# A hybrid decoder step on one core: seven of twelve pairs of expert weight chunks stored as 32 KB rows and loaded by one 4 MB transfer each

## The reference

```python
xn  = rmsnorm(x)
mix = x + (sum_i sigmoid(gate_i) * (branch_i @ w_br_i)) @ w_o    # three branches from xn @ w_in
xn2 = rmsnorm(mix)
grp = argmax(xn2 @ w_rg + b_rg)            # one of 4 groups
top2 of the 8 experts of the group, weight = p(group) * softmax(top2 logits)
for each of 32 experts e:
    h    = silu(xn2 @ w_gate[e]) * (xn2 @ w_up[e])     # 2048 -> 512
    out += (h * combine[:, e]) @ w_down[e]             # 512 -> 2048
y = rmsnorm(mix + out)
```

## Time and profile before

| | |
|---|---|
| time, median of 3 runs | 1625.97 us (1625.96 to 1627.1) |
| span of the profiled execution | 1624.0 us |
| PE busy | 1412.6 us, 87% |
| DVE, ACT busy | 563.5 us, 408.6 us |
| DMA moved | 544.69 MB, mean 335 GB/s |
| chain that ended last | DMA 49%, PE 48% |

### The profile page before, as it was taken

The page is one execution under the profiler, slowest core; times in us unless marked ns, Lnnn a source line. Parts: engine busy times, 40 slices in busy tenths (PEclk is TensorE's granted clock), DMA queues, the critical chain, the costliest instruction groups (busy, mean ns, idle before and its releaser), DMA issues.

```text
span 1624.0 us, 24618 instructions
## 1 busy us (share of the span) xinstructions
PE 1412.6 (87%) x10019; PEld 931.0 (57%) x10019; DVE 563.5 (35%) x924; ACT 408.6 (25%) x684; POOL 29.9 (2%) x52
## 2 busy tenths in 40 slices
PE   7999999999999999999877777877878867967866
PEld 7999999999999999953322322322312412412311
DVE  5647765554455555442111111112111111201204
ACT  6454344333333344321201101002002002002003
POOL 0100020000000010000000000000000000000000
PEclk9999999999999999999989989989889989989989
DMA  8776555545555558699999999999999999999997
GB/s 334 291 299 240 168 164 182 182 158 203 181 181 181 194 218 354 240 360 423 428 426 429 429 426 428 429 429 427 428 428 429 428 427 429 428 427 429 429 427 307
DMA packets 53022, 544.69 MB, mean 335 GB/s; under 512 B 6289, under 2 KB 6337, under 8 KB 11609
## 3 DMA queue, kind: packets, MB, share of 16 engines
q1 hardware_dynamic: 51442, 539.26, 82.1%
q0 software_dynamic: 1392, 4.78, 1.1%
q10 hardware_dynamic: 144, 0.02, 0.0%
HBM read 540.30 MB, written 3.68 MB: 335 GB/s over the span
## 4 chain that ended last, share of the span: by engine, by line
DMA 49%; PE 48%; DVE 1%; ACT 1%; issue 0%; SPq 0%; DVEq 0%; ACTq 0%
DMA trunk<-in_expert_chunks 27%; DMA ring<-in_expert_chunks 18%; PE bank L1468 13%; PE bank L1469 13%; PE bank L1470 13%; PE bank L1860 4%; DMA side<-in_expert_chunks 3%; PE bank L1863 1%; DMA ring<-in_dense_units 1%; PE bank L1746 1%; PE bank L1630 0%; PE bank L1792 0%; DMA trunk<-in_mem_cols 0%; PE bank L1800 0%; PE bank L1664 0%
## 5 line engine op out<-in xcount | busy, mean ns | idle before, releaser
L940 DVE TENSOR_TENSOR w_lo<-ring,w_hi 128x1024 fp32r<-128x1024 f32 x220 | 259.8, 1222 | 223.2 <-ACT w_hi L673 222.7
L1468 PE MATMUL bank<-xn_hi,w_hi 128*128 128x264 f32 x1120 | 319.0, 285 | 0.0
L1469 PE MATMUL bank<-xn_lo,w_hi 128*128 128x264 f32 x1120 | 317.3, 283 | 0.0
L1470 PE MATMUL bank<-xn_hi,w_lo 128*128 128x264 f32 x1120 | 317.1, 283 | 0.0
L673 ACT ACTIVATE w_hi<-ring 128x1024 fp32r<-128x1024 f32 x220 | 221.1, 1052 | 366.5 <-PE bank L1470 333.1
L1468 PEld LDWEIGHTS bank<-xn_hi,w_hi 128*128 128x128 f32 x1120 | 210.9, 188 | 1.1 <-issue 1.0
L1469 PEld LDWEIGHTS bank<-xn_lo,w_hi 128*128 128x128 f32 x1120 | 211.1, 188 | 0.1
L1470 PEld LDWEIGHTS bank<-xn_hi,w_lo 128*128 128x128 f32 x1120 | 210.0, 187 | 0.0
L1860 PE MATMUL bank<-ring,trunk 128*32 128x512 f32 x896 | 125.6, 685 | 55.4 <-DMA ring<-in_expert_chunks 55.4
L1860 PE MATMUL bank<-side,trunk 128*32 128x512 f32 x832 | 118.7, 694 | 58.1 <-DMA side<-in_expert_chunks 56.7
L1746 PEld LDWEIGHTS bank<-trunk,x_all 128*128 128x128 f32 (+1 forms) x672 | 93.3, 192 | 75.7 <-issue 55.8
(11 more groups left out here) (324 smaller groups left out, 1730.7 us busy)
## 6 DMA issues: line engine op xcount, KB each, us to landing
ring<-in_expert_chunks SPq DMA_DIRECT2D x79, 2048.0 KB, 37.0
side<-in_expert_chunks SPq DMA_DIRECT2D x72, 2048.0 KB, 36.3
ring<-in_dense_units SPq DMA_DIRECT2D x109, 1024.0 KB, 4.8
trunk<-in_expert_chunks SPq DMA_DIRECT2D x24, 2048.0 KB, 36.9
trunk<-in_expert_chunks SPq DMA_DIRECT2D x16, 1024.0 KB, 38.8
side<-in_expert_chunks SPq DMA_DIRECT2D x16, 1024.0 KB, 40.8
x_all<-in_k_cols SPq DMA_DIRECT2D x8, 512.0 KB, 7.7
x_all<-in_cache_mem_v SPq DMA_DIRECT2D x8, 512.0 KB, 6.6
```

The lines of the kernel that those rows point to most:

```text
L940: V.tensor_tensor(w_lo[n % 2][:, js, :], raw[n % 2][:, js, :], w_hi[n % 2][:, js, :], ALU.subtract).then_inc(lo_done, 1)
L1468: mm(ps[:, 0:n], w_hi[b][:, j, :], x_hi[:, j, :], start=j == k0, stop=False)
L1469: mm(ps[:, 0:n], w_hi[b][:, j, :], x_lo[:, j, :], start=False, stop=False)
L1470: ins = mm(ps[:, 0:n], w_lo[b][:, j, :], x_hi[:, j, :], start=False, stop=j == k1 - 1)
```

## The change

On the host, the two chunks of seven pairs of each round (0 and 1, 4 and 5, 6 and 7, 8 and 9, 12 and 13, 16 and 17, 20 and 21) are interleaved by partition: in HBM a partition's 16 KB of one chunk are followed by its 16 KB of the other, so a pair is 128 rows of 32 KB. Their two slots lie side by side in SBUF (for the pairs with the value 1 in `PAIRS` in the reverse order), and one transfer of 128 x 32 KB fills both. It is issued when the second of the two earlier chunks is used, since it overwrites both. PE waits once, before the first chunk of a pair, for the whole pair. The other ten chunks of a round are loaded as before, and so are five places in the first round: chunk 4, the halves of 5, chunks 6, 7, 8 and 9 come singly, as 16 KB or 8 KB pieces out of the 32 KB rows. The pair 0, 1 of the first round is one transfer at k = 3; nothing is issued at k = 5 any more.

The diff:

```diff
--- before.py
+++ after.py
@@ -57,8 +57,10 @@
 CREDIT = 8
 SLOT = [EORDER[c % 8] for c in range(CPR)]
 SLOT[14], SLOT[15], SLOT[22], SLOT[23] = 8, SLOT[6], SLOT[7], 8
-REFILL = [(p, p + 8) for p in range(6)] + [(None, 14), (6, 15)] + [(p, p + 8) for p in range(8, 14)] + [(None, 22), (14, 23)]
-AHEAD = [(16 + c, c) for c in range(6)] + [(None, 6), (22, 7)]
+PAIRS = {0: 0, 4: 1, 6: 0, 8: 0, 12: 1, 16: 0, 20: 1}
+SECOND = {c + 1: c for c in PAIRS}
+REFILL = [(1, 8), (2, 10), (3, 11), (5, 12), (None, 14), (6, 15), (9, 16), (10, 18), (11, 19), (13, 20), (None, 22), (14, 23)]
+AHEAD = [(17, 0), (18, 2), (19, 3), (21, 4), (22, 6)]
 SP_STEPS = (0, 6, 7, 8, 14, 15, 16, 22, 23)
 
 
@@ -366,6 +368,7 @@
         e_used, p_ready, p_step, silu_done, h_ready, y_ready = (
             sem("e_used"), sem("p_ready"), sem("p_step"), sem("silu_done"), sem("h_ready"), sem("y_ready"))
         sq_done, f_var, f_sqrt, f_rms = sem("sq_done"), sem("f_var"), sem("f_sqrt"), sem("f_rms")
+        first4_in, first6_in, first8_in = sem("first4_in"), sem("first6_in"), sem("first8_in")
         half_full, acc2_in, shift_ok, spread_ok = sem("half_full"), sem("acc2_in"), sem("shift_ok"), sem("spread_ok")
         g_ready, g_taken, half0_full = sem("g_ready"), sem("g_taken"), sem("half0_full")
         first_turned, first_taken = sem("first_turned"), sem("first_taken")
@@ -383,14 +386,16 @@
 
         def expert_full(c):
 
-            return sum(32 if k == 14 else 16 for k in range(c + 1) if SLOT[k] == SLOT[c])
+            return sum(32 if k == 14 else 16 for k in range(c + 1) if SLOT[k] == SLOT[c] and k not in SECOND)
 
         def slot_fills(c):
 
-            return expert_full(max(k for k in range(CPR) if SLOT[k] == SLOT[c]))
+            return expert_full(max(k for k in range(CPR) if SLOT[k] == SLOT[c] and k not in SECOND))
 
         units_v = dense_units.rearrange("m p n -> p m n")
         chunk_v = expert_chunks.rearrange("r c p n -> p c r n")
+        pair_v = expert_chunks.rearrange("r (q t) p n -> r q (t p n)", t=2).rearrange("r q (p m) -> p q r m", p=P)
+        pair_slot = {4: view(side, 4096, 2 * CHUNK), 1: view(ring, 0, 2 * CHUNK), 3: view(ring, UNIT0, 2 * CHUNK)}
 
         raw = [view(ring, b * KT * P, KT, P) for b in range(2)]
 
@@ -478,12 +483,24 @@
                              chunk_v[:, c, round_of, jj * (CHUNK // 2):(jj + 1) * (CHUNK // 2)]).then_inc(
                                  half_full if c == CPR - 1 and jj else full[8], 16)
 
+            def from_pair(c, round_of, n0, n1):
+
+                c0 = SECOND.get(c, c)
+                at = (c - c0 ^ PAIRS[c0]) * CHUNK
+                return pair_v[:, c0 // 2, round_of, at + n0:at + n1]
+
+            def one_of_pair(c, round_of, signal):
+
+                sp.dma_start(e_slot[SLOT[c]].rearrange("p (o n) -> p o n", o=1), from_pair(c, round_of, 0, CHUNK)).then_inc(signal, 16)
+
             def expert_load(c, round_of):
 
                 s = SLOT[c]
                 if s == 8:
                     half_load(c, 0, round_of)
                     half_load(c, 1, round_of)
+                elif c in PAIRS:
+                    sp.dma_start(pair_slot[s].rearrange("p (o n) -> p o n", o=1), pair_v[:, c // 2, round_of, :]).then_inc(full[s], 16)
                 else:
                     sp.dma_start(e_slot[s].rearrange("p (o n) -> p o n", o=1), chunk_v[:, c, round_of, :]).then_inc(full[s], 16)
 
@@ -504,20 +521,22 @@
                     if k == 2:
                         sp.wait_ge(x_zero, 1)
                         sp.dma_start(g_row, g_final.rearrange("(o n) -> o n", o=1)).then_inc(gfin_in, 16)
-                    if 3 <= k < 3 + 2 * EARLY and k % 2:
-                        expert_load(k // 2 - 1, slice(0, 1))
+                    if k in (3, 7, 9):
+                        expert_load({3: 0, 7: 2, 9: 3}[k], slice(0, 1))
+                    if k == 11:
+                        one_of_pair(4, slice(0, 1), first4_in)
 
             sp.wait_ge(aux_ready, A_O + KT - 4)
             sp.wait_ge(lg_ready, KT // 2 - 2)
             residual(KT - 2)
-            for half, signal in ((0, half0_full), (1, full[SLOT[EARLY]])):
+            for half, signal in ((0, half0_full), (1, full[SLOT[4]])):
                 sp.wait_ge(*lo_after(N_OUT + 14 + half))
                 cols = slice(half * (CHUNK // 2), (half + 1) * (CHUNK // 2))
                 sp.dma_start(e_slot[SLOT[EARLY]][:, cols].rearrange("p (o n) -> p o n", o=1),
-                             chunk_v[:, EARLY, slice(0, 1), cols]).then_inc(signal, 16)
-            for c in (1, 2):
-                sp.wait_ge(z_ready, Z_END + c - 2)
-                expert_load(EARLY + c, slice(0, 1))
+                             from_pair(EARLY, slice(0, 1), cols.start, cols.stop)).then_inc(signal, 16)
+            for c, signal in ((6, first6_in), (7, full[SLOT[6]])):
+                sp.wait_ge(z_ready, Z_END + c - 7)
+                one_of_pair(c, slice(0, 1), signal)
             half_load(14, 0, slice(0, 1))
             sp.wait_ge(aux_ready, A_LT + 1)
             half_load(14, 1, slice(0, 1))
@@ -536,7 +555,11 @@
                     expert_load(c, of_round)
 
             with sp.Fori(0, npass) as k:
-                refill(REFILL, k * (ROUNDS * CPR) + CREDIT, slice(0, 1), 14)
+                sp.wait_ge(e_used, k * (ROUNDS * CPR) + (CREDIT + 1))
+                one_of_pair(8, slice(0, 1), first8_in)
+                sp.wait_ge(e_used, k * (ROUNDS * CPR) + (CREDIT + 2))
+                one_of_pair(9, slice(0, 1), full[SLOT[8]])
+                refill(REFILL[1:], k * (ROUNDS * CPR) + CREDIT, slice(0, 1), 14)
                 refill(AHEAD, k * (ROUNDS * CPR) + CREDIT, slice(1, 2))
                 with sp.Fori(1, ROUNDS - 1) as r:
                     refill(REFILL, k * (ROUNDS * CPR) + r * CPR + CREDIT, bass.ds(r, 1))
@@ -1764,6 +1787,7 @@
             pe.wait_ge(np_ready, 1)
             npass = pe.value_load(npass_i[0:1, 0:1], min_val=1, max_val=9)
             pe.wait_ge(half0_full, 16)
+            pe.wait_ge(first4_in, 16)
             pe.wait_ge(first_taken, 1)
             with pe.Fori(0, npass) as k:
                 with pe.Fori(0, ROUNDS) as r:
@@ -1845,7 +1869,12 @@
                                 ins = tr(ps[:, j * P:(j + 1) * P], h[:, j, :], ident[:, :])
                             ins.then_inc(aux_ready, 1)
                             pe.wait_ge(aux_done, it * JPR + (A_E + JOB_H + 1))
-                        pe.wait_ge(full[SLOT[c]], it * slot_fills(c) + expert_full(c))
+                        if c == 6:
+                            pe.wait_ge(first6_in, 16)
+                        if c == 8:
+                            pe.wait_ge(first8_in, k * 16 + 16)
+                        if c not in SECOND:
+                            pe.wait_ge(full[SLOT[c]], it * slot_fills(c) + expert_full(c))
                         for jj in range(2):
                             w = weights(SLOT[c], jj)
                             if jj and c < 8:
@@ -1876,6 +1905,18 @@
          (1, 8, 1, 768)]
 
 
+def interleave_pairs(out):
+
+    import numpy as np
+
+    for c, last_first in PAIRS.items():
+        both = out[:, c:c + 2].transpose(0, 2, 1, 3)
+        if last_first:
+            both = both[:, :, ::-1]
+        out[:, c:c + 2] = np.ascontiguousarray(both).reshape(ROUNDS, 2, P, CHUNK)
+    return out
+
+
 def pack_experts(w_gate, w_up, w_down):
 
     import numpy as np
@@ -1887,7 +1928,7 @@
         into[:, 8 * i:8 * i + 8] = w.transpose(0, 2, 4, 3, 1, 5)
     w = np.asarray(w_down).reshape(ROUNDS, EPR, 2, 2, P, 4, 512)
     into[:, 16:].reshape(ROUNDS, 4, 2, P, 2, EPR, 512)[:] = w.transpose(0, 5, 2, 4, 3, 1, 6)
-    return out
+    return interleave_pairs(out)
 
 
 def columns(*rows):
```

## The result

The changed kernel takes 1630.53 us (median of 16 runs), the kernel before 1626.01 us (16 runs): a ratio of 1.0031 with a 95% interval of 1.0024 to 1.0037. It is slower by 4.5 us. The forecast was 1628.7 within 1623.8 to 1632.8, with 0.45 on slower by over 0.2%.

The account below looks back on a forecast made before the run. PE was taken to bound the kernel up to 700 us, DMA streaming from about 730. Terms +1.05 +1.45 -3.5 +2.6 +1.1 = +2.7 us took the span from 1624.0 to 1626.7, median 1628.7 us, range 1623.8 to 1632.8.

Parts of the forecast that it names:

- The other signs: Expected in the new profile: 117.1 us rounds; last half of chunk 23 without a wait, ending 14.6 us after pair 20, 21.
- case 1: The forecast itself: four small terms, three of them losses, nearly cancel; 1628.7 us, own range 1627.0 to 1630.5, chance 0.55.
- What a byte costs: Expert stream: 32 KB rows and one transfer save 0.07 us per pair, 50 pairs, -3.5 us, bounds 0 and -5.5.
- Rival 2: Each of the 50 pairs: a long row saves nothing, leaving losses of +6.2 us, 1632.2 us; chance 0.2.
- rival 4: Expert stream: longer rows stream slower, 0.1 us lost on each of 53 pairs, +11.5 us, 1637.5 us; chance 0.05.
- The dense part: Unit at k = 4 lands later behind 4 MB and PE stalls once, +1.05 us, bounds 0 and 2.
- The dry gaps: First round: pairs 12, 13 and 16, 17 are issued later, DMA runs dry twice, +1.45 us, bounds 0.8 and 2.
- The later rounds: After the first round: later issue of pairs costs nothing, since five or six chunks are still queued.
- Rival 5: Later rounds: DMA runs dry there too, at 1 us per pair, 1680 us; chance 0.03.
- The tail: Last round: PE has more work after pair 20, 21 lands, +2.6 us; slower clock after idling, +1.1, bounds 0 and +2.
- Rival 3: Losses smaller than worked out and 32 KB rows save 0.11 us: 1622 to 1624 us or little more; chance 0.15.
- rival 6: The change does not do what it says, each pair moves as before; in time like Rival 2; chance 0.02.

Follow-up runs that it names:

- rows16: Changed kernel with the same transfers, but a pair's chunks one behind the other in HBM, so 256 rows of 16 KB per pair: 1635.44 us.
- spaced: Kernel before with its loads unchanged, but read from the changed kernel's HBM layout: 1626.34 us.
- first profile: Profiled run of the unmodified changed kernel, its fastest at 1626.63 us; the second profile is a later run of it, 1632.95 us.
- first_single: Changed kernel with chunks 0 and 1 of the first round loaded as two transfers at k = 3 and 5: 1628.12 us.
- dry_only: Kernel best with chunks 12, 13 and 16, 17 of the first round as pairs again: 1624.35 us.
- best: Changed kernel with chunks 0, 1, 12, 13, 16, 17 of the first round and 16, 17, 20, 21 of the last loaded singly: 1622.36 us.
- tail_only: Kernel best with chunks 16, 17 and 20, 21 of the last round as pairs again: 1626.32 us.
- keep_less: Changed kernel with 14 unused small matmuls added before PE's wait for the pair 16, 17: 1629.69 us.

## Why the prediction was right, and where it was off

The time was inside the range, and each of its five terms was found at its place with its sign. The other signs came too: 117.1 us a round, and a last half of chunk 23 that waits for no landing and ends 14.3 us after the last pair's, forecast 14.6. The median lies 1.8 us above the forecast, past the 0.2% line on the side that had 0.45. Of the rivals case 1, four small terms, describes the mechanism, but the median lies at the edge of that case's own range of 1627.0 to 1630.5, and the 1631.1 of all 22 runs beyond it. Part of the nearness is luck: between medians the losses measured 9.0 us together where 6.2 were forecast, and the gain 4.0 where 3.5, so the errors partly cancel in the total.

- **What a byte costs.** Forecast -3.5 (0.07 per pair), measured 0.074 x 50, that is -3.7. The step that inferred a 32 KB row's saving from the 8 KB rows of the split chunks was sound, though for half of its stated reason: part of it was put down to one transfer instead of two, and rows16 shows that this part is nil. Rival 2 (no saving) and rival 4 (longer or wider rows stream slower) fall.
- **What a page has for it.** The trace has 9 ns a row. The Trainium skill ("DMA: Bandwidth & Descriptors", section Bandwidth, Why small descriptors are slow) gives about 3 cycles per packet, 3.5 ns by my estimate from that page; the two differ, and the measurement decides. For the pitch, spaced shows no loss with rows 32 KB apart; the warning of the Trainium skill ("DMA: Bandwidth & Descriptors", section Latency and other measured facts, HBM row pitch at large powers of two), whose figures start at 512 KiB, does not reach down to here.
- **The dense part.** Forecast +1.05, bounds 0 and 2. The mechanism and place were right (0.58 us stall and a first refill 0.8 later in the first profile). The size was too small: first_single puts it at 3.0 us between the medians, with 1.5 to 5.1 open, and the traces show 0.8 to 2.4 for the stall. One thing was missing for certain, a landing that comes 1.5 us later in some runs. Whether the half clock near 618 and 710 belongs to it is open, as it followed one of three stalls of 2 us and also stands near 710 without any stall.
- **The dry gaps.** Forecast +1.45 (the forecast's own landings, 758.04 and 756.49, give 1.55), measured 1.5 in the first profile's first round, 2.0 between dry_only and best. Single profiles can't tell this term: spaced, with the loads of before, has a first round of 79.5 us, 1.2 longer than before and nearly that of dry_only. The 9.2 us from issue to landing that the forecast took as fixed vary as well: the first refill of the expert part, also issued into an empty queue, landed 9.0 us later before the change, 8.7 and 7.5 in the two profiles of the changed kernel, and 7.2 in best. The two dips of the DMA share that the forecast named are shallow: 0.88 over 729 to 731 us and over 748 to 750, where before has 1.06 and 1.01.
- **The later rounds.** Forecast: nothing. Rounds 1 to 7 take 809.8 to 810.3 us with 50 or so pairs against 814.9: 5.1 less, of which the pairs explain 3.7. Rival 5 (dry in later rounds) falls. The other 1.4 us are in rows16 too (813.4, without any saving by rows), and in spaced (813.5, without any pair), so they are no effect of the change but two pauses in the one profile that the forecast started from. In the kernel before, two landings come 0.7 and 0.8 us late, at 801.3 and 1537.2; the changed kernel has none such. Beside both stands an 8 KB instruction load of queue q14, here the second (packets, MB, share of 16 engines, 1535 to 1537.2 us):

```profile
q1 hardware_dynamic: 63, 0.97, 104.2%
q14 instruction: 1, 0.01, 0.9%
```

  The changed kernel has one such load at 828 with no delay beside it, and spaced, whose transfers are those of before, has two, at 799.5 and 1535.4, with none. So the load alone does not bring the delay, and its cause stays open.
- **The tail.** Forecast +2.6 for the order and +1.1 for the clock, together 3.7; tail_only against best measured 4.0. The order's part is as forecast (13.3 us in keep_less against 13.5). The clock's part is 1.0 in the first profile, 5.6 in the second (14.3 and 18.9 less 13.3). The forecast took 1.6 us lost from rows after 3.8 us of idle, but after 5 us of idle the half clock lasted for up to 12.7 us of work. The bound of +2 for it was too tight.
- **The sum.** With the parts as measured between medians: best is 4.0 below before; tail 4.0, dry gaps 2.0 and first pair 3.0 give +5.0, where the changed kernel has +4.5 in its first 16 runs, and +4.5 again if all 22 (1631.1) are set against all 31 runs of before (1626.6). With 3.0 for the first pair open by two microseconds either way, the sum is consistent but proves no single term.

The tail's clock term and the first round's missing one have one root. The forecast was made from one profile of before, which holds no idle of PE longer than 3.8 us in the expert part, no half clock before 821 us and no stall in the dense part. The terms that the clock feeds also differ from run to run, so the median lies above a sum that is made for one good run. Rival 3 and rival 6 did not come in.
